# Eight of nineteen input-projection chunks per layer from split rows and weights, the weights' low part summed by a GpSimd transfer

## The reference

```python
def hybrid_layer(h, ...):
    n = rmsnorm(h, g_mix)
    z = n @ w_in                        # 1024 -> 2432 columns: the input projection
    y_a = gate_b * causal_dwconv(gate_c * xa, prev_a, w_conv_a)      # group A, 384
    zb = gelu(z[..., o3:o4]); u = zb[..., :D_B]                      # group B, 256
    v = layernorm(zb[..., D_B:], g_ln_b, b_ln_b)
    y_b = u * chunk_mix(v, w_s, b_s)
    y_c = silu(layernorm(causal_dwconv(glu(zc)) + b, ...))           # group C, 384
    h = h + concat(rmsnorm(y_a), rmsnorm(y_b), rmsnorm(y_c)) @ w_o
    h = h + ffn(rmsnorm(h, g_ffn))      # layer 0: dense SwiGLU; layer 1: top 2 of 8 experts
    h = h + sigmoid(rmsnorm(h, g_ple) @ w_ple_gate) * (p_i @ w_ple_proj)
```

## Time and profile before

| | us |
|---|---|
| median of 3 runs | 1088.12 (1087.45 to 1088.53) |
| the profiled execution, its own time | 1089.55 |
| its span in the profile | 1087.9 |
| layer 0's input projection on PE | up to 79.24 |
| layer 1's input projection on PE | up to 412.23 |
| PE busy | 1065.3 |
| DVE busy | 900.1 |
| granted TensorE clock, mean | 0.995 |

### The profile page before, as it was taken

One profiled execution on the slowest core, in us unless ns is written; L12 is line 12 of the kernel. 1 busy time (PEld: TensorE's weight loads), 2 busy tenths in 40 slices (PEclk: granted clock), 3 DMA queues, 4 the chain that ended last, 5 costly groups with the idle time before them and its releaser, 6 DMA issues.

```text
span 1087.9 us, 16254 instructions
## 1 busy us (share of the span) xinstructions
PE 1065.3 (98%) x5883; PEld 922.3 (85%) x5883; DVE 900.1 (83%) x1284; ACT 674.9 (62%) x857; POOL 45.2 (4%) x58
## 2 busy tenths in 40 slices
PE   9998999999999998999999999999999999999996
PEld 8887999999999887888888888888888888878786
DVE  5899866566678988659989899898998999999785
ACT  2106544345454115458788888888888878887674
POOL 1000000000000000000000010100100001002100
PEclk9999999999999999999999999999999999999998
DMA  8342645545444433429999999999999999999911
GB/s 336 150 155 80 232 163 208 215 163 210 170 155 155 159 108 138 155 93 386 363 372 397 351 408 354 370 407 355 392 369 358 398 367 385 374 365 417 368 76 40
DMA packets 24197, 291.50 MB, mean 268 GB/s; under 512 B 3160, under 2 KB 3192, under 8 KB 7376
## 3 DMA queue, kind: packets, MB, share of 16 engines
q1 hardware_dynamic: 21040, 280.32, 67.2%
q0 software_dynamic: 3104, 10.46, 2.8%
HBM read 283.98 MB, written 6.79 MB: 267 GB/s over the span
## 4 chain that ended last, share of the span: by engine, by line
PE 92%; DVE 3%; DMA 2%; ACT 2%; issue 1%; POOL 0%; DVEq 0%; ACTq 0%; POOLq 0%
PE bank L667 15%; PE bank L713 15%; PE bank L671 15%; PE bank L670 15%; PE bank L737 8%; PE bank L740 8%; PE bank L741 8%; DMA ring<-wstream 2%; PE bank L753 2%; DVE wlo L1296 1%; PE bank L611 1%; PE bank L576 1%; PE bank L595 1%; ACT whi L904 0%; PE bank L775 0%
## 5 line engine op out<-in xcount | busy, mean ns | idle before, releaser
L1296 DVE TENSOR_TENSOR wlo<-ring,whi 128x1024 fp32r<-128x1024 f32 x384 | 460.0, 1221 | 50.6 <-ACT whi L904 44.0
L904 ACT ACTIVATE whi<-ring 128x1024 fp32r<-128x1024 f32 x384 | 404.5, 1059 | 86.8 <-PE bank L667 69.5
L667 PE MATMUL bank<-whi,gh_hi 128*128 128x512 f32 x512 | 204.3, 399 | 0.1
L671 PE MATMUL bank<-whi,gh_lo 128*128 128x512 f32 x512 | 199.8, 390 | 0.0
L670 PE MATMUL bank<-wlo,gh_hi 128*128 128x512 f32 x512 | 199.5, 390 | 0.0
L737 PE MATMUL bank<-gh_hi,whi 128*128 128x264 f32 x480 | 138.0, 288 | 0.2 <-issue 0.2
L740 PE MATMUL bank<-gh_lo,whi 128*128 128x264 f32 x480 | 136.0, 283 | 0.0
L741 PE MATMUL bank<-gh_hi,wlo 128*128 128x264 f32 x480 | 135.9, 283 | 0.0
L667 PEld LDWEIGHTS bank<-whi,gh_hi 128*128 128x128 f32 x512 | 96.2, 188 | 21.9 <-DVE wlo L1296 3.5
L671 PEld LDWEIGHTS bank<-whi,gh_lo 128*128 128x128 f32 x512 | 96.1, 188 | 20.9
L670 PEld LDWEIGHTS bank<-wlo,gh_hi 128*128 128x128 f32 x512 | 96.3, 188 | 18.4
(11 more groups left out here) (268 smaller groups left out, 1384.0 us busy)
## 6 DMA issues: line engine op xcount, KB each, us to landing
ring<-wstream SPq DMA_DIRECT2D x130, 2048.0 KB, 8.3
y_rows<-work POOLq DMA_DIRECT2D x7, 512.0 KB, 8.2
ring<-wstream SPq DMA_DIRECT2D x1, 1536.0 KB, 10.3
h<-x_in SPq DMA_DIRECT2D x2, 528.0 KB, 4.0
y_out<-work SPq DMA_DIRECT2D x2, 528.0 KB, 3.0
par<-par_in SPq DMA_DIRECT2D x2, 494.5 KB, 6.8
c_sample<-xc POOLq DMA_DIRECT2D x2, 372.0 KB, 3.8
stc<-state_in SPq DMA_DIRECT2D x2, 360.0 KB, 9.4
```

The costliest lines, as they stand in the source:

```text
L667: mm = pe.matmul(out[:, :], xh, whi[:, pos, cols_], start=(k == 0), stop=False)
L671: mm = pe.matmul(out[:, :], xl, whi[:, pos, cols_], start=False, stop=(k == last))
L904: nc.scalar.activation(whi[:, q % SPLITS, :], quarter_at(q), ACT.Copy).then_inc(S["hi"], 1)
L1296: v.tensor_tensor(wlo[:, q % SPLITS, :], quarter_at(q), whi[:, q % SPLITS, :].bitcast(F32), ALU.subtract).then_inc(S["lo"], 1)
```

## The change

The last eight of the 13 `zab` chunks of each layer (`SUM_FROM = 5`: zab 5 to 12; their quarters are `SUM_Q`) go by `project` instead of `project_fp32`. For them:

- **Rows.** At the start of each layer ACT writes eight `gh_hi` (rounding copies of `gz[k]`), and DVE eight `gh_lo` (`gz[k]` minus `gh_hi`).
- **Weights.** ACT writes `whi` as before and also `wlo = -1 x quarter`, rounded to fp32r, the negated high part. Then GpSimd issues a transfer that adds the ring's quarter onto `wlo` (`accum_op=add`, 512 KB). DVE has no part in it. PE waits for the landing (`low_landed`), and so does SP before it overwrites the ring's slot.
- **Queues.** GpSimd issues five of the eight transfers ahead of `v_sample`'s wait for the scaled rows, three behind it. On ACT `high_upto` brings the copies of the changed quarters up to three chunks ahead of PE; the last three quarters' copies stand behind the wait for `scaled` and the scaling (L1042 before, L1105 after).
- `ones_ready` is merged into `consts`, and the semaphores of the `wo` rows' parts into `rows_hi` and `rows_lo`.

```diff
+SUM_FROM = 5
+SUM_Q = [NEED[_b["zab"] + _c] - 1 for _b in BASE for _c in range(SUM_FROM, N_ZAB)]
 def in_fp32(q):
-    return any(0 <= q - a < n for a, n in zip(FP32_FROM, FP32_Q))
+    return q not in SUM_Q and any(0 <= q - a < n for a, n in zip(FP32_FROM, FP32_Q))
...
+def landings(q):
+    return 16 * sum(s <= q and place_of(s) == place_of(q) for s in SUM_Q)
...
                 if whole:
                     sp.wait_ge(acc_ready, sum(n <= whole[-1] + 1 for n in NEED))
-                if len(whole) < QUARTERS:
-                    sp.wait_ge(dense["lo"], splits(qs.stop))
+                for q in qs:
+                    if q in SUM_Q:
+                        sp.wait_ge(low_landed[place_of(q)], landings(q))
+                if any(q not in SUM_Q and not in_fp32(q) for q in qs):
+                    sp.wait_ge(dense["lo"], by_vector(qs.stop))
...
+            def add_weights(l, end):
+                for c in range(summed[0], end):
+                    q = NEED[BASE[l]["zab"] + c] - 1
+                    at = place_of(q)
+                    pool.wait_ge(minus_high, by_transfer(q) + 1)
+                    pool.dma_start(wlo[:, at, :], quarter_at(q), accum_op=ALU.add).then_inc(low_landed[at], 16)
+                summed[0] = end
+            B_EARLY = 2 * CB + 6
...
+                add_weights(l, B_EARLY)
                 pool.wait_ge(S["ln_b"], CB)
                 pool.dma_start(v_sample[l], lnb[:, :, SEQ:T]).then_inc(stored, 16)
+                add_weights(l, N_ZAB)
...
+                            if w == 0 and q in SUM_Q:
+                                pe.wait_ge(low_landed[place_of(q)], landings(q))
+                            elif w == 0:
+                                pe.wait_ge(S["lo"], by_vector(q) + 1)
...
+                def zab_chunks(first, n):
+                    for c in range(first, first + n):
+                        if c < SUM_FROM:
+                            project_fp32(B["zab"] + c, 1, gz)
+                        else:
+                            project(B["zab"] + c, 1, *ghs, rows_lo if c == SUM_FROM else None, waited=KD * 2 * l)
...
                     nc.scalar.activation(whi[:, at, :], quarter_at(q), ACT.Copy).then_inc(S["hi"], 1)
+                    if S is dense and q in SUM_Q:
+                        nc.scalar.activation(wlo[:, at, :], quarter_at(q), ACT.Copy, scale=-1.0).then_inc(minus_high, 1)
...
+                act.wait_ge(S["gh_mix"], KD)
+                if l:
+                    act.wait_ge(acc_ready, BASE[0]["ple"] + KD)
+                for k in range(KD):
+                    nc.scalar.activation(gh_hi[:, k, :], gz[k], ACT.Copy).then_inc(rows_hi, 1)
...
                 root_of(bank[5], root[:, :], (S["variance"], 1), S["root_v"])
+                high_upto(dense_quarters(B["zab"] + 2 * CB + 2))
                 act.wait_ge(S["scaled"], 1)
...
+                    if S is dense and q in SUM_Q:
+                        continue
                     dve.wait_ge(S["hi"], i + 1)
...
+                for k in range(KD):
+                    dve.wait_ge(rows_hi, KD * 2 * l + k + 1)
+                    nc.vector.tensor_tensor(gh_lo[:, k, :], gz[k], gh_hi[:, k, :].bitcast(F32),
+                                            ALU.subtract).then_inc(rows_lo, 1)
```

More of the change, by code:

```diff
@@ L144, in splits, with by_vector, by_transfer, place_of @@
     return sum(s < q for s in SPLIT_Q)
+def by_vector(q):
+    return sum(s < q for s in SPLIT_Q if s not in SUM_Q)
+def by_transfer(q):
+    return sum(s < q for s in SUM_Q)
+def place_of(q):
+    return (splits(q) + SPLIT_AT) % SPLITS
+def landings(q):
+    return 16 * sum(s <= q and place_of(s) == place_of(q) for s in SUM_Q)
 def dense_quarters(chunk):
@@ L294, in build @@
         late_step = sem("overflow_step")
+        minus_high = sem("minus_high_written")
+        low_landed = [sem(f"weights_added_to_minus_high_{i}") for i in range(SPLITS)]
+        rows_hi, rows_lo = sem("high_parts_of_rows"), sem("low_parts_of_rows")
         L = [{n: sem(f"{n}_{l}") for n in (
@@ L302, in build @@
             "y_c", "y_a", "y_b", "ys_sq", "y_ms", "y_root", "y_normed", "sq_ffn",
-            "gh_ple", "sq_ple", "sig_ple", "tails", "w_sT", "y_hi", "y_lo")} for l in range(DEPTH)]
+            "gh_ple", "sq_ple", "sig_ple", "tails", "w_sT")} for l in range(DEPTH)]
         L[0].update({n: sem(n) for n in ("gh_ffn", "silu", "hid_f32", "hid_hi", "hid", "hid2")})
@@ L419, in _ @@
             for d, t in ones.items():
-                pool.memset(t[:, :], 1.0 / d).then_inc(ones_ready, 1)
+                pool.memset(t[:, :], 1.0 / d).then_inc(consts, 1)
             pool.memset(eps[:, :], EPS).then_inc(consts, 1)
@@ L716, in project_fp32, with project @@
                     mm.then_inc(acc_ready, 1)
-            def project(first_chunk, n_chunks, hi, lo, waits=None, S=dense, after=None):
+            def project(first_chunk, n_chunks, hi, lo, waits=None, S=dense, after=None, waited=0):
                 for i in range(n_chunks):
@@ L727, in project @@
                         q, w = divmod(at[0], QBLOCKS)
[L728 to L733, removed]
+                        if S is not dense:
+                            if w == 0:
+                                pe.wait_ge(S["lo"], q + 1)
+                        else:
[3 more added lines that the diff above has]
+                                pe.wait_ge(S["lo"], by_vector(q) + 1)
+                            q = splits(q) + SPLIT_AT
                         if i == 0 and waits:
-                            pe.wait_ge(waits, k + 1)
+                            pe.wait_ge(waits, waited + k + 1)
                         wh, wl = block_of(S, q, w)
@@ L772, in _ @@
             mix = both(hid_hi, hid_lo, KD)
-            pe.wait_ge(ones_ready, len(ones))
+            pe.wait_ge(consts, len(ones))
             for _ in range(WARM_UP):
                 pe.matmul(bank[7][:, 0:P], ones[1][:, :], ones[1][:, :], start=True, stop=True)
-            pe.wait_ge(consts, 13)
+            pe.wait_ge(consts, 17)
             for l in range(DEPTH):
                 S, B = L[l], BASE[l]
+                def zab_chunks(first, n):
+                    for c in range(first, first + n):
+                        if c < SUM_FROM:
+                            project_fp32(B["zab"] + c, 1, gz)
+                        else:
+                            project(B["zab"] + c, 1, *ghs, rows_lo if c == SUM_FROM else None, waited=KD * 2 * l)
                 if l == 0:
@@ L784, in _ @@
                 project_fp32(B["zc"] + 1, N_ZC - 1, gz)
-                project_fp32(B["zab"], 2 * CB, gz)
+                zab_chunks(0, 2 * CB)
                 average(bank[5], D_B, [zb[:, c, :] for c in range(CB)], S["mean"], (S["gelu"], 1))
-                project_fp32(B["zab"] + 2 * CB, 2, gz)
+                zab_chunks(2 * CB, 2)
                 pe.wait_ge(S["squared"], 1)
                 average(bank[5], D_B, [sq[:, c, :] for c in range(CB)], S["variance"])
-                project_fp32(B["zab"] + 2 * CB + 2, 3 * CA - 2, gz)
+                zab_chunks(2 * CB + 2, 3 * CA - 2)
                 pe.wait_ge(S["ln_b"], CB)
@@ L830, in _ @@
                     else:
-                        project(B["wo"] + k, 1, *mix, S["y_lo"] if k == WO_FP32 else None)
+                        project(B["wo"] + k, 1, *mix, rows_lo if k == WO_FP32 else None, waited=KD * (2 * l + 1))
                     if l and k:
@@ L1081, in _ @@
                     act.wait_ge(S["y_normed"], k + 1)
-                    nc.scalar.activation(hid_hi[:, k, :], ycat[:, k, :], ACT.Copy).then_inc(S["y_hi"], 1)
+                    nc.scalar.activation(hid_hi[:, k, :], ycat[:, k, :], ACT.Copy).then_inc(rows_hi, 1)
                 for k in range(KD):
@@ L1425, in add_to_h @@
                 dve.wait_ge(acc_evac, chunk + 1)
-            dve.wait_ge(consts, 13)
+            dve.wait_ge(consts, 17)
             dve.wait_ge(par_loaded[0], 16)
```

11 lines of the change are left out of this document (6 added, 5 removed).

## The result

The changed kernel takes 1107.38 us (median of 4 runs, 1105.57 to 1107.82) against 1088.32 for the kernel before in the same comparison: 1.0173 times as long, 95% interval 1.0157 to 1.0189. It is slower by 19 us, above the forecast of 1089.1 and above its range (1082 to 1102). The profiled execution took 1107.03 us with a span of 1105.3, 17.4 over the span before.

A forecast was written before the change was run, and what follows sets the result against it. PE was taken to bound the kernel, DVE just behind; PE's gain of 5.1 us a layer was to be paid back by waits for `wlo`, leaving 1088.12 + 1.0 = 1089.1 us, range 1082 to 1102.

The forecast's parts named there:

- parts 1 and 2: Changed chunks: PE's matmuls 2.92 for 3.56 us, 5.1 a layer less; DVE's pace limits the gain to 3.5 a layer, 7.0.
- Part 3: Row splits on ACT (2.60 us) and DVE (2.83) at each layer's start: cost nothing, at most 1 us in layer 1.
- Part 4: ACT's copies for eight quarters, 17.5 us, delaying gelu steps by up to 2.2 each: counted nothing, at most 0.5 a layer.
- Part 5: Adding transfers: 2.66 us of data each, landing 4.6 in quiet, 9.4 beside a ring load, against 6.6 allowed; +1.0 net.
- a sum over the stretch: DMA engines' work before the last chunk: +0.1 or +0.8 us in layer 0, +0.2 to +2.7 in layer 1; +1.0 taken.
- rival 3: PE waits of 2 us and more drop the clock, 1.75 us a fall: 1092.5 to 1096; chance 0.10 together with another rival.
- rival 2: Each transfer late, PE waiting for wlo at every changed chunk, from about 2.8 us of data: 1102 to 1110; chance 0.23.
- Rival 4: Three late pairs behind ACT's scaling held by DVE's slipping `scaled`, 2 us a layer: 1093; chance 0.10 together with another rival.
- rival 1: Transfers land in time at 1.23 to 2.3 us each, DVE's ceiling decides: -2.9 to -7, 1081 to 1085.5; chance 0.33.

The follow-up runs named there:

- e1: The changed kernel without its adding transfers, GpSimd only passing the signal on, ACT's second copy writing zeros: 1080.99 us.
- e3: The changed kernel with the three ring loads of each layer beside the adding transfers cut to 64 KB: 1083.23 us.
- e6: The changed kernel with six spread chunks a layer (zab 5, 6, 8, 9, 11, 12), ACT's copies started up to six quarters ahead: 1082.57 us.
- e10: The changed kernel with only the last six chunks a layer in a row (zab 7 to 12), copies three chunks ahead: 1098.61 us.
- e9: The changed kernel with useless PE matmuls (4 to 10) ahead of the five chunks before which it waited: 1103.04 us.
- e2: The changed kernel with adding transfers of a quarter of their size (128 KB), ACT's second copy writing zeros: 1086.64 us.
- e7: The changed kernel with 8 to 20 useless PE matmuls ahead of the five chunks, twice as long as the waits: 1116.41 us.
- e8: The changed kernel with plain copies of the same bytes in place of the adding transfers: 1089.16 us, one run.
- e4: The changed kernel with the low parts made by a GpSimd subtraction, without ACT's negated copy or any transfer: 1110.46 us.

## Why the prediction was wrong

- **What bounds the kernel, parts 1 and 2: right.** A changed chunk takes 2.92 us of matmuls, and the ceiling of 7.0 us without late landings was measured at 7.1 (e1). PE gives part of its gain back behind the stretch, in a wait of 1.8 us for DVE.
- **Part 3, the rows' parts: right.** In layer 1 the fp32 chunk zab 4 begins at 384.96 and in layer 0 at 46.98, 337.98 apart; that is the old 332.99 and layer 0's 5.0. The splits cost nothing. The sign that the prediction gave ("wrong if layer 1's chunk zab 4 ends later than 332.99 us after layer 0's") was a poor one: a loss in layer 0's own stretch sets it off too, as here.
- **Part 4, ACT's copies: right** in e1, where nothing of them is seen.
- **Part 5, the price of one transfer: right.** 2.66 us of data were taken and 2.7 measured; a quiet landing was put at 4.6 and is 4.5 to 5.2 with no other transfer ahead of it (e3). The reckoning of a landing beside a ring load, 9.4 against 6.6 us of budget, is what happened too: the median of all 16 was 9.8.
- **Part 5, the step that failed**: "Since single landings overlap, I count what the DMA engines must move". I had the late landing in hand and let a sum over the stretch overrule it. That sum is a floor, since it takes the engines as always fed. Here a transfer can't be issued before its buffer is free, and so PE's waits follow from the landing against the 8.8 us of lead. PE waited 6.7 and 12.3 us, 19.0 in both layers, where the sum had 11.2 (the 10.2 of part 1 paid back, and 1.0). In layer 0, where the engines were full, the sum missed least: the first data came at 46.3 and not at 43, because the start beside a ring load takes over 4 us and not 1.6. In layer 1 they were at 0.78 and the sum was of no use. e6 and e10 bear it out: the same bytes with more lead, and further apart, cost next to nothing.
- **The clock, left out of the forecast.** It stood apart as rival 3, with a chance shared of 0.10, as if waits of 2 to 5 us could come without it. The forecast put it at nothing, and yet it had about 5 us a layer of PE's waits; the price of 1.75 us a fall, from the earlier trace rows, was right in the mean (1.7 to 1.8), and five falls make 8.8 us. e9 shows that the falls need the standstill; why three waits of 1.9 to 3.3 us (e2, e10, e7) had none is open.
- **The rivals.** The time is rival 2's (1102 to 1110), its mechanism only in part: its point was 2.8 us of data a transfer, and the transfers took 2.7. PE stood ahead of 5 of 16 chunks. Rivals 2 and 3 were one case: late landings, 8 us more of waits than forecast and 9 of clock. Rival 4, the three late pairs behind the scaling, is seen only in e3, at 1.1 and 1.5 us. In rival 1 the end of 2.9 us counts one layer; with 2.3 us a transfer the two layers and the forecast's 1.0 make -4.8, so 1083.3 and not 1085.5.
- **The Trainium skill's fit** ("DMA: Bandwidth & Descriptors", section "Anatomy of one DMA — SWDGE (gpsimd) path") gives 3.2 us for such a transfer, an estimate from that page. e3 has 4.5 in quiet, so for an adding one the fit is 1.3 short; the fastest plain copy of e8 landed in 3.2, so there the trace agrees. The Trainium skill also says there, in the section "SWDGE vs HWDGE vs iDMA", that a DMA engine serves its queues in turn. Where both queues had packets, the trace bears it out: 128 packets of a transfer then took 4.9 to 6.5 us in the changed kernel, in place of 2.8 to 2.9. For the first 4 to 5 us it can't tell: the window from 380.7 to 385.7 has none of GpSimd's packets, and nothing shows whether they already stood there to be served.

What stays open: why a transfer's first packet comes so late beside a ring load. No run tells whether the packets or what they are made from are held up.

## What to carry to other kernels

Where work is handed to a transfer, set the landing, at its worst and beside the other queues' traffic, against the time from "buffer free" to "wanted"; the total of bytes over the stretch only says what is impossible. If the landing is longer, fewer and more spread transfers with an earlier start can keep nearly the whole gain (e6: 6.9 of 7.1 us, with 12 transfers in place of 16). And where a sum has TensorE wait for some us at a time, put a fall of the clock on top (here 1.75 us in the mean): each of the waits over 4 us had one, and about half of those between 1.8 and 3.3.

## What the runs showed of the hardware

- An adding transfer of 512 KB from SBUF to SBUF keeps the DMA engines busy for 2.7 us, the same as a plain copy 1.4 (e8).
- Beside a 2 MB load, GpSimd's 512 KB transfer had no packet for 4.0 to 5.1 us after its issue, one of 128 KB for 3.4 to 4.8 (e2); with the loads cut short and no other transfer ahead it was 1.4 to 1.5 (e3).
- A GpSimd subtraction of 128x1024 took 2.6 us and held one DVE instruction on SBUF data beside it for as long: a tap of 0.4 us took up to 2.62, a product of 128x8 2.36 for 0.16. The other taps kept their pace (e4).
- Behind each of PE's five waits of 1.9 to 4.9 us in the changed kernel the clock fell to 1.2 GHz, at a loss of 1.7 to 1.8 us in the mean. Behind waits of 0.9 and 1.0 us it did not (e9), nor behind one of 1.9 (e2), 2.0 (e10) and 3.3 us (e7).
